# Neighbourhood attention in token tiles of 16 rows x 8 columns in a hybrid encoder block

## The chip, the core and the metric

The kernel runs on one core of a Trainium2 chip. Its engines are TensorE (PE in the profile, its weight loads PEld), VectorE (DVE), ScalarE (ACT), GpSimd (POOL) and SyncE (SP), which here only issues transfers. The metric is the time of one execution on the device in microseconds (us), the median of several runs.

## The reference

One layer of an encoder is applied to two groups of tokens with shared weights: a prompt of 1024 tokens (a grid of 16 rows x 64 columns) and a sample of 256 tokens (4 rows x 64 columns), 1024 features each. What matters here:

```python
kh = min(NA_KH, rows)                     # 8 of the 16 rows; all 4 of the sample
row_start = jnp.clip(r - kh // 2, 0, rows - kh)
key_rows = row_start[:, None] + jnp.arange(kh)[None, :]
col_start = jnp.clip(c - NA_KW // 2, 0, GRID_W - NA_KW)      # 16 of the 64 columns
in_win = (c[None, :] >= col_start[:, None]) & (c[None, :] < col_start[:, None] + NA_KW)
s = jnp.einsum('rqhd,rikhd->hrqik', qg, kg).astype(jnp.float32) * scale + bias
s = jnp.where(mask, s, -jnp.inf)
```

So a token attends to 8 rows x 16 columns around it, in 8 heads of 64, with a learned bias by relative row and column. The second half of the features goes through differential attention (4 heads, every token sees every token of its group, with a T5 bucketed bias by the distance of the token numbers). Both halves are normalised per head, concatenated and multiplied by `w_out`; then follow a mixture of 16 experts, each of which takes the tokens with the best router values (128 of the prompt, 32 of the sample), and a last norm.

## The kernel before

The work is written by hand as one program per engine with semaphores between them; the order on each engine is the order of the code. Tokens are handled in tiles of 128: tiles 0 to 7 are the prompt, 8 and 9 the sample. In the kernel before, a prompt tile is two grid rows of 64 columns, so tile t is tokens 128t to 128t + 127.

Stages: (1) x tiles are loaded, normalised (VectorE), turned (TensorE transposes) and the values of the neighbourhood heads are projected; (2) neighbourhood attention, steps s = 0 to 39, step s = job s // 10 (two heads), tile s % 10; (3) the values of the differential heads are projected; (4) differential attention, steps 40 to 79; (5) `w_out`, the second norm and the router, tile by tile; (6) choice of tokens for each expert; (7) the 16 experts, from about 865 us to the end.

A step s of stage 2 on TensorE is: `scores(s)` (three matmuls for each head, queries and keys split into a high and a low part; L709), `values(s - 2)` (L747), half of a projection part of the next job (`project_part`, L644 to L646), the transposes of the exponentials of step s - 1 (`turn_exps`, L639), the other half of the projection part, and one transpose of an output (`out_turn`). VectorE adds the bias and takes the maximum (`na_bias`, `bias_max`, L1525), ScalarE takes the exponential (L1173), copies the transposes out (L1184), and rounds a finished projection part (`proj_round`, L1152), which VectorE then splits (`proj_lows`, L1507). The parts share one PSUM bank, so the next part's first matmul waits for that split. Parts of 512 columns end at tiles 1, 3, 6 and 8, parts of 256 at tiles 4 and 9.

The window of a tile is in `na_window`: 512 keys for tiles 0, 1, 6 and 7, 576 for tiles 2 to 5 (nine grid rows), 256 for the sample. The bias of two heads stands in a table TE (128 partitions x 2 heads x 16 rows x 64 columns), read with an offset by the tile; a second form TI serves the tiles with 576 keys. A table is loaded by SyncE in four transfers from the DRAM tensor `bias_rows` (`na_table`, L537), and GpSimd adds the column mask and makes TI (`bias_tables`, L1970 to L1980). The T5 bias is one row of 2047 values for each head; GpSimd writes it to DRAM 128 times, each shifted by one (`t5_shifted`, L2024), and SyncE loads one table of 128 x 1920 for each head (`df_table`, L540).

SyncE's queue is one list: weights of a projection (`unit`, tile `w_st`, one buffer, L503; each waits until the one before it is split) and the tables, in the order of the code. In stage 5 SyncE loads for each tile the x rows (L577) and the mixed rows (L580), and GpSimd stores the residual and the normalised rows (L2088, L2090). In stage 6 TensorE counts the places of the chosen tokens with bf16 matmuls (`count`, L897).

## Time and profile before

| | us |
|---|---|
| median of three runs | 2776.01 (2773.64 to 2778.3) |
| the profiled execution | 2778.91 |
| its span | 2777.2 |

| engine | busy us | share | instructions |
|---|---|---|---|
| TensorE, matmuls | 2681.3 | 97% | 22988 |
| TensorE, weight loads | 2524.0 | 91% | 22988 |
| VectorE | 1979.2 | 71% | 2352 |
| ScalarE | 1716.1 | 62% | 2562 |
| GpSimd | 1110.5 | 40% | 745 |

Busy times of engines overlap, so they don't add up to the span. A matmul's duration in the trace reaches over the start of the next one, since matmuls are pipelined; what one costs is read from start to start. The experts take about 1912 us of the span, the neighbourhood attention (stage 2) 237 us.

### The profile page before, as it was taken

Reading aid. Unit: us, or ns where it says so; the run is one execution under the profiler, and the core shown is the slowest. Engines: PE = TensorE matmul, PEld = TensorE weight load, DVE = VectorE, ACT = ScalarE, POOL = GpSimd, SP = SyncE. Lnnn points to the kernel's source line nnn. Section 1 sums busy time; section 2 is a strip of 40 time slices with the busy share of each in tenths; the row PEclk is TensorE's granted clock in tenths of the full one; section 3 lists DMA queues with packets and bytes.
Section 4 is the critical chain, followed back from the end, with each engine's and each line's share of the span. In section 5 each row is a group of like instructions: output and inputs, shape, how many; then the busy total and the mean of one; then the engine's idle time right before and its main releaser. Section 6 shows DMA issues by size and latency. Waiting matters only on the chain. (4 is left out here: it accounts for less than half of the span.)

```text
span 2777.2 us, 54444 instructions
## 1 busy us (share of the span) xinstructions
PE 2681.3 (97%) x22988; PEld 2524.0 (91%) x22988; DVE 1979.2 (71%) x2352; ACT 1716.1 (62%) x2562; POOL 1110.5 (40%) x745
## 2 busy tenths in 40 slices
PE   7999999998986999999999999999999999999997
PEld 7887898877876999999999999999999999999997
DVE  5233326666367878878788787888878788787877
ACT  3366615555114676767667676676767767676675
POOL 2132220124112443636446273552635436263455
PEclk9999999999997999999999999999999999999999
DMA  7231110113364888889887898879889888898987
GB/s 188 54 101 40 48 55 30 40 56 102 127 239 143 316 289 316 285 318 315 290 325 265 318 316 308 317 267 342 285 310 323 287 307 286 318 316 305 320 284 290
DMA packets 357643, 655.40 MB, mean 236 GB/s; under 512 B 25751, under 2 KB 85015, under 8 KB 356887
## 3 DMA queue, kind: packets, MB, share of 16 engines
q1 hardware_dynamic: 341291, 606.41, 61.4%
q0 software_dynamic: 16112, 45.53, 6.1%
q8 instruction: 183, 3.00, 0.4%
q14 instruction: 57, 0.47, 0.0%
HBM read 616.48 MB, written 39.62 MB: 236 GB/s over the span
## 5 line engine op out<-in xcount | busy, mean ns | idle before, releaser
L1798 DVE TENSOR_TENSOR wl<-stg,wh 128x2048 bf16<-128x2048 f32 (+1 forms) x544 | 1244.3, 2292 | 270.4 <-ACT wh L1312 265.7
L1312 ACT ACTIVATE wh<-stg 128x2048 fp32r<-128x2048 f32 (+1 forms) x544 | 1010.9, 1861 | 204.4 <-PE S L958 77.9
L2160 POOL TENSOR_TENSOR hx<-hh,hx 128x320 fp32r<-128x320 f32 x176 | 385.1, 2188 | 811.7 <-ACT hx L1365 811.5
L955 PE MATMUL S<-X,wh 128*128 128x320 f32 x3760 | 593.1, 313 | 1.3 <-DVE X L1807 1.3
L955 PEld LDWEIGHTS S<-X,wh 128*128 128x128 f32 x3760 | 557.5, 189 | 3.9 <-issue 2.1
L1001 PE MATMUL S<-hx,wh 128*128 128x320 f32 x1892 | 312.4, 313 | 5.3 <-DVE yTs L1846 5.2
L955 PE MATMUL OG<-X,wh 128*128 128x320 f32 x1872 | 298.5, 312 | 0.7 <-DVE gg L1828 0.7
L958 PE MATMUL S<-Xb,wl 128*128 128x160 bf16 x3760 | 290.1, 233 | 0.0
L1001 PEld LDWEIGHTS S<-hx,wh 128*128 128x128 f32 x1892 | 280.7, 188 | 7.4 <-issue 7.1
L955 PEld LDWEIGHTS OG<-X,wh 128*128 128x128 f32 x1872 | 277.2, 188 | 2.1 <-issue 1.9
L958 PEld LDWEIGHTS S<-Xb,wl 128*128 128x128 bf16 x3760 | 258.9, 98 | 12.0
L2162 POOL CAST hb<-hx 128x320 bf16<-128x320 f32 x176 | 206.1, 1171 | 0.0
L1365 ACT ACTIVATE hx<-hh 128x320 fp32r<-128x320 f32 x176 | 83.1, 472 | 176.3 <-DVE hh L1835 176.3
L1999 POOL TENSOR_TENSOR ca<-lsum,half 128x20 f32<-128x20 f32 (+3 forms) x10 | 24.2, 2420 | 395.1 <-ACT o_all L1205 242.5
L1001 PE MATMUL OG<-hx,wh 128*128 128x320 f32 x924 | 158.0, 313 | 1.9 <-DVE yTs L1846 1.9
L958 PE MATMUL S<-hb,wl 128*128 128x160 bf16 x1892 | 158.8, 233 | 0.0
L1173 ACT ACTIVATE E<-E,nmax 128x1024 f32<-128x1024 f32 (+1 forms) x80 | 81.8, 1023 | 109.9 <-DVE nmax L1525 109.9
L644 PE MATMUL OG<-hT_h,wkq 128*128 128x512 f32 (+1 forms) x384 | 149.2, 388 | 0.1
L958 PE MATMUL OG<-Xb,wl 128*128 128x160 bf16 x1872 | 149.2, 233 | 0.0
L1001 PEld LDWEIGHTS OG<-hx,wh 128*128 128x128 f32 x924 | 138.7, 188 | 2.5 <-issue 2.5
L958 PEld LDWEIGHTS S<-hb,wl 128*128 128x128 bf16 x1892 | 132.1, 98 | 8.1
L646 PE MATMUL OG<-hT_h,wkq 128*128 128x512 f32 (+1 forms) x384 | 136.8, 356 | 0.0
(287 smaller groups left out, 4277.5 us busy)
## 6 DMA issues: line engine op xcount, KB each, us to landing
stg<-in_w_gate_dram SPq DMA_DIRECT2D x80, 2048.0 KB, 8.7
stg<-in_w_up_dram SPq DMA_DIRECT2D x80, 2048.0 KB, 9.5
stg<-in_w_down_dram SPq DMA_DIRECT2D x64, 2048.0 KB, 12.0
stg<-in_w_down_dram SPq DMA_DIRECT2D x32, 1536.0 KB, 11.4
stg<-in_w_gate_dram SPq DMA_DIRECT2D x16, 1024.0 KB, 5.2
stg<-in_w_up_dram SPq DMA_DIRECT2D x16, 1024.0 KB, 5.2
w_st<-in_w_in_dram SPq DMA_DIRECT2D x20, 512.0 KB, 3.7
yt<-mixed SPq DMA_DIRECT2D x10, 512.0 KB, 4.5
```

Of the source, the lines that this page charges most:

```text
L644: pe.matmul(out, lhs_h, rhs_h, start=first, stop=False)
L646: return pe.matmul(out, lhs_l, rhs_h, start=False, stop=last)
L955: pe.matmul(out, w, x, start=first, stop=False, skip_group_check=True)
L958: return pe.matmul(out[:, 0:CT], w, x, start=False, stop=last, skip_group_check=True)
L1001: mm = pe.matmul(down_bank(e, d), whk[:, f, c * P:(c + 1) * P], hx[:, f0 + f, :], start=(f0 + f == 0), stop=(last and f0 + f == FT - 1), s ...
L1173: act.activation(e, e, ACT.Exp, scale=-1.0, bias=nmax[:, col:col + 1], accum_out=lsum[:, j % 2, t, hf:hf + 1]).then_inc(exp_done, 1)
L1312: act.activation(piece_conv(wh, g), piece_stage(g), ACT.Copy).then_inc(rounded, 1)
L1365: act.activation(hx[:, j - 1:j + 1, 0:CT], hh[:, :, :], ACT.Copy).then_inc(hidden_hi, 1)
L1798: dve.tensor_tensor(piece_conv(wl, g), piece_stage(g), piece_conv(wh, g).bitcast(F32), ALU.subtract).then_inc(split, 1)
L1999: own(pool.tensor_tensor(a, ls, minus_one, ALU.pow))
L2160: pool.tensor_tensor(hx[:, f, CT:2 * CT], hh[:, :, :], hx[:, f, 0:CT].bitcast(F32), ALU.subtract).then_inc(hidden_ready, 1)
L2162: pool.tensor_copy(hb[:, f, :], hx[:, f, 0:CT].bitcast(F32)).then_inc(hidden_b, 1)
```

## The change

Prompt tiles are cut another way: tile t is the 16 rows of the grid by the 8 columns 8t to 8t + 7, so partition 8r + c holds row r, column 8t + c. The 16 columns that a token attends to lie in its own tile and the two beside it, so a window is 384 keys for tiles 1 to 6 and 256 for tiles 0 and 7. The sample keeps its tiles. All layouts of prompt tokens follow: x rows are loaded and the residual and normalised rows are stored by these tiles (`octet`, `octet_of`), the two DRAM tensors stay in the token order.

- Bias of the neighbourhood heads: `na_table` now loads, for each head, two pieces TS for the sample (64 x 6 x 64) and 16 pieces TR, one for each query row (8 partitions x 8 x 24), 36 transfers a table. GpSimd masks TS and makes from TR five blocks TB (left, own, right tile, with and without a column mask for the outer ones).
- Bias of T5: GpSimd reads the T5 rows back as 32 partitions of 2040, puts them into the new order with 15 copies of 32 x 248 (`t5_w`) and stores them in 8 transfers (`t5_octets`). `df_table` loads 16 pieces for each head, one for each grid row. The shifted table stays for the sample alone, much smaller (`df_sample_table`). VectorE's first bias waits for the 8 stores too, since `t5_w` lies under its output.
- VectorE makes one more mask (`window_mask`): five small operations more in the load stage.
- Mixed rows: `mixed_rows(t)` issues the mixed rows as soon as their buffer is free, and the x rows behind them, each with a semaphore of its own; before, x rows stood ahead and both waited for `x2_ready`.
- Choice of tokens: the counting on TensorE uses two more matrices (`row_le`, `row_lt`) so that equal router values go in token order; 32 count matmuls instead of 18. `list_constants` on GpSimd makes them, and the token numbers of the new tiles.
- Weights of the projection (5, 0) are now loaded before the wait for the values of stage 3.

Cut to its core, the diff is:

```diff
 def na_window(t):
     if t >= TPR:
-        return TPR, NSA, 7 - 2 * (t - TPR), False
-    if t < 2:
-        return 0, 512, 7 - 2 * t, False
-    if t < 6:
-        return t - 2, 576, 3, True
-    return 4, 512, 3 - 2 * (t - 6), False
+        return TPR, NSA
+    first, last = max(t - 1, 0), min(t + 1, TPR - 1)
+    return first, (last - first + 1) * P
...
             def na_table(j):
                 for hh_ in range(2):
+                    q = (2 * j + hh_) * NDR
                     for up in range(2):
-                        q = (2 * j + hh_) * NDR
-                        src = G_d[:, q:q + NDR, GW - 1:2 * GW - 1]
-                        sp.dma_start(TE[j % 2][GW * up:GW * up + GW, hh_, up:up + NDR, :], src).then_inc(te_in[j % 2], 16)
+                        sp.dma_start(TS[j % 2][GW * up:GW * up + GW, hh_, :, :],
+                                     G_d[:, q + 5 - up:q + 11 - up, GW - 1:2 * GW - 1]).then_inc(te_in[j % 2], 16)
+                    for r in range(GR):
+                        r0 = row_start(r)
+                        d0 = q + r0 - r + NA_KH - 1
+                        sp.dma_start(TR[j % 2][OC * r:OC * r + OC, hh_, r0:r0 + NA_KH, :],
+                                     G_d[0:OC, d0:d0 + NA_KH, GW - 1 - OC:GW - 1 + 2 * OC]).then_inc(te_in[j % 2], 16)
             def df_table(h):
-                sp.dma_start(BT[h % 2][:, :], Fs_d[h, :, P - 1:P - 1 + 1920]).then_inc(bt_in[h % 2], 16)
+                for r in range(GR):
+                    sp.dma_start(BT[h % 2][OC * r:OC * r + OC, :].rearrange("c (g q) -> c g q", q=P),
+                                 W_d[h, :, :, GR - 1 - r:2 * GR - 1 - r, :].rearrange("c g r k -> c g (r k)")
+                                 ).then_inc(bt_in[h % 2], 16)
...
             def mixed_rows(t):
+                if t < 2:
+                    x_again(t)
                 if t >= 2:
                     sp.wait_ge(turned, wo_fill["y", t - 2] + 2)
-                    sp.wait_ge(x2_ready, t - 1)
-                sp.dma_start(xt[:, t % 2, :], x_rows(t)).then_inc(y_in[t % 2], 16)
                 if t % 4 == 0:
                     sp.wait_ge(y_rest_stored[t // 4], 16)
                 sp.dma_start(yt[t % 2][:, :], y_d[t * P:(t + 1) * P, :]).then_inc(y_in[t % 2], 16)
+                if t >= 2:
+                    x_again(t)
...
             def window_mask():
                 dve.wait_ge(const_ready, 1)
+                dve.wait_ge(ident_ready, 1)
+                own(dve.tensor_tensor_reduce(msk_j[:, :], identf[:, :], msk_c[:, :], 1.0, 0.0, ALU.mult, ALU.add,
+                                             col_of[:, :]))
+                own.wait()
+                own(dve.tensor_tensor(from_col[:, :], msk_c[:, 0:OC], col_of[:, :].to_broadcast([P, OC]), ALU.is_ge))
+                own.wait()
+                dve.tensor_scalar(mask_lr[:, 0, :], from_col[:, :], -MASKED, MASKED, ALU.mult, ALU.add)
+                dve.tensor_scalar(mask_lr[:, 1, :], from_col[:, :], MASKED, 0.0, ALU.mult, ALU.add)
...
+            for g in range(2 * TPR - 1):
+                own(pool.tensor_copy(t5_w[:, g, :, :], t5_x[:, OC * g:OC * g + (2 * GR - 1) * GW].rearrange(
+                    "q (r w) -> q r w", w=GW)[:, :, 0:OC]))
+            own.wait()
+            for c in range(OC):
+                pool.dma_start(W_d[:, c].rearrange("h g r k -> h (g r k)"),
+                               t5_w[OC - 1 - c:DF_H * OC:OC].rearrange("q g r k -> q (g r k)")).then_inc(W_out, 16)
...
+            for t in range(TPR):
+                if t + 1 < TPR:
+                    n = TPR - t - 1
+                    count(ranks[:, 0, t + 1:TPR, :], one, chosen[:, 0, t, :].unsqueeze(1).to_broadcast([P, n, NE]))
+                    count(ranks[:, 1, t + 1:TPR, :], row_le, chosen[:, 1, t, :].unsqueeze(1).to_broadcast([P, n, NE]))
+                if t:
+                    count(ranks[:, 1, 0:t, :], row_lt, chosen[:, 1, t, :].unsqueeze(1).to_broadcast([P, t, NE]))
+                count(ranks[:, 1, 0:TPR, :], one, chosen[:, 0, t, :].unsqueeze(1).to_broadcast([P, TPR, NE]))
```

How this moves instructions, at three places. First TensorE in stage 2, from the end of one step to the values of the next, in job 0. S is the score bank, OG holds outputs and projections, PT the transposes, En the exponentials, PTs their copies. Before (a step with 576 keys):

```order
L639 MATMUL PT<-identf,En 128x128
L639 MATMUL PT<-identf,En 64x128
L639 MATMUL PT<-identf,oTs 128x128
L709 MATMUL S<-K_h,Qh 128x288 x2
L709 MATMUL S<-K_l,Qh 128x288 x2
L709 MATMUL S<-K_h,Ql 128x288 x2
L709 MATMUL S<-K_h,Qh 128x288 x2
L709 MATMUL S<-K_l,Qh 128x288 x2
L709 MATMUL S<-K_h,Ql 128x288 x2
L747 MATMUL OG<-PTs,V 64x128 x10
```

and now (384 keys):

```order
L689 MATMUL PT<-identf,En 128x128 x6
L694 MATMUL OG<-hT_h,wkq 128x512
L695 MATMUL OG<-hT_l,wkq 128x512
L696 MATMUL OG<-hT_h,wkq 128x512
L694 MATMUL OG<-hT_h,wkq 128x512
L695 MATMUL OG<-hT_l,wkq 128x512
L696 MATMUL OG<-hT_h,wkq 128x512
L689 MATMUL PT<-identf,oTs 128x128
L759 MATMUL S<-K_h,Qh 128x384 x2
L759 MATMUL S<-K_l,Qh 128x384 x2
L759 MATMUL S<-K_h,Ql 128x384 x2
L795 MATMUL OG<-PTs,V 64x128 x6
```

The scores are one group of three pairs, the third group of transposes behind the second half of the projection is gone, and six value matmuls stand for ten.

Second SyncE's queue around the first tables, where `w_st` is the buffer of projection weights. Before:

```order
L503 DMA w_st<-in_w_in_dram 128x8x128 [waits w_split] x2
L537 DMA TE_71<-bias_rows 64x15x64 [waits te_clear,G_out]
L537 DMA TE_71<-bias_rows 64x15x64 x3
L537 DMA TE_72<-bias_rows 64x15x64 x4
L503 DMA w_st<-in_w_in_dram 128x8x128 [waits w_split] x3
```

and now:

```order
L529 DMA w_st<-in_w_in_dram 128x8x128 [waits w_split] x2
L562 DMA TS_73<-bias_rows 64x6x64 [waits te_clear,G_out]
L562 DMA TS_73<-bias_rows 64x6x64
L567 DMA TR_75<-bias_rows 8x8x24 x16
L562 DMA TS_73<-bias_rows 64x6x64 x2
L567 DMA TR_75<-bias_rows 8x8x24 x16
L562 DMA TS_74<-bias_rows 64x6x64 x2
L567 DMA TR_76<-bias_rows 8x8x24 x16
L562 DMA TS_74<-bias_rows 64x6x64 x2
L567 DMA TR_76<-bias_rows 8x8x24 x16
L529 DMA w_st<-in_w_in_dram 128x8x128 [waits w_split] x3
```

Between the same two weight loads stand 72 transfers instead of 8.

Third GpSimd between the store of the T5 rows (`t_rows`) and the first table. Before:

```order
L1956 DMA t_rows<-t_p 4x2048 [waits t5_ready]
L1959 MEMSET TE_71 128x2048 [waits va_split,const_dma]
L1960 MEMSET TE_72 128x2048
L1961 TENSOR_SCALAR slw<-slw 128x128
L1970 TENSOR_TENSOR TE_71<-TE_71,mask 128x2048 [waits pool_own,mask_ready,te_in0]
```

and now:

```order
L2028 DMA t_rows<-t_p 4x2048 [waits t5_ready]
L2031 MEMSET TR_75 128x768 [waits va_split,const_dma]
L2032 MEMSET TR_76 128x768
L2033 TENSOR_SCALAR slw<-slw 128x128
L2042 DMA t_x<-t_rows 32x1x2040 [waits pool_own,squared,F_out,turned]
L2046 COPY t_w<-t_x 32x248 [waits shifts_in]
L2046 COPY t_w<-t_x 32x248 x14
L2050 DMA t_octets<-t_w 4x3720 [waits pool_own]
L2050 DMA t_octets<-t_w 4x3720 x7
L2060 TENSOR_TENSOR TS_73<-TS_73,mask 128x768 [waits te_in0,mask_ready]
```

The read, the 15 copies and the 8 stores stand ahead of the first table's mask.

## Rows read from the trace of the kernel before

**Rows 1.** Stretch: length; busy PE, PEld, DVE, ACT, POOL; clock; DMA share; GB/s.

```profile
112.90:350.30 237.40, 236.32 (x1903) 189.42 (x1902) 74.59 (x203) 153.12 (x520) 58.06 (x42) 1.00 0.21 57
830.00:865.00 35.00, 6.82 (x47) 5.40 (x48) 24.21 (x77) 8.71 (x12) 8.64 (x12) 0.50 0.06 19
```

**Rows 2.** Timeline of TensorE, 131 to 137 us: 576 keys (start, duration, engine, line).

```profile
131.12 1.03 PE L639 MATMUL PT<-identf,En 128*128 128x128 f32 x8
131.91 0.47 PE L644 MATMUL OG<-hT_h,wkq 128*128 128x512 f32 x1
...
133.37 0.38 PE L639 MATMUL PT<-identf,En 128*128 128x128 f32 x2
133.59 0.27 PE L639 MATMUL PT<-identf,oTs 128*128 128x128 f32 x1
133.79 0.40 PE L709 MATMUL S<-K_h,Qh 64*128 64x288 f32 x2
...
134.78 1.46 PE L747 MATMUL OG<-PTs,V 128*64 128x128 f32 x20
136.17 0.38 PE L644 MATMUL OG<-hT_h,wkq 128*128 128x256 f32 x1
```

**Rows 3.** Timeline of TensorE, 224 to 232 us: 256 and 512 keys.

```profile
224.46 0.39 PE L709 MATMUL S<-K_h,Qh 64*128 64x256 f32 x2
...
225.01 1.09 PE L747 MATMUL OG<-PTs,V 128*64 128x128 f32 x16
226.04 0.39 PE L644 MATMUL OG<-hT_h,wkq 128*128 128x256 f32 x1
...
227.57 0.60 PE L639 MATMUL PT<-identf,En 128*128 128x128 f32 x4
227.92 0.36 PE L644 MATMUL OG<-hT_h,wkq 128*128 128x256 f32 x1
...
229.64 0.50 PE L709 MATMUL S<-K_h,Qh 64*128 64x512 f32 x2
...
230.54 0.66 PE L747 MATMUL OG<-PTs,V 128*64 128x128 f32 x8
231.13 0.50 PE L644 MATMUL OG<-hT_h,wkq 128*128 128x512 f32 x1
```

**Rows 4.** Timeline at 121 us: last projection matmul, the next weights' rounding, the split.

```profile
121.30 0.39 PE L646 MATMUL OG<-hT_h,wkq 128*128 128x512 f32 x1
...
122.22 0.62 ACT L1113 ACTIVATE wkq<-w_st 128x512 fp32r<-128x512 f32 x1
...
122.36 0.69 DVE L1507 SCALAR_TENSOR_TENSOR K_l<-OG,K_h 128x512 fp32r<-128x512 f32 x1 [3.15 <-ACT K_h L1152]
```

**Rows 5.** Timeline of SyncE's queue, and landings: KB each, median us to landing.

```profile
35.19 0.43 SPq L526 DMA_DIRECT2D lam_v<-in_lambda_k_dram  x1
...
78.95 9.13 SPq L537 DMA_DIRECT2D TE<-bias_rows  x8
...
167.25 2.84 SPq L537 DMA_DIRECT2D TE<-bias_rows  x4
...
w_st<-in_w_in_dram SPq DMA_DIRECT2D x20, 512.0 KB, 3.7
```

**Rows 6.** Timeline of GpSimd, 50 to 92 us; in brackets idle time and what ended it.

```profile
55.63 0.63 POOL L1956 DMA_DIRECT2D t_rows<-t_p  x1 [8.01 <-DVE t_p L1402]
...
87.50 4.60 POOL L1970 TENSOR_TENSOR TE<-TE,mask 128x2048 f32<-128x2048 f32 x1 [27.11 <-DMA TE<-bias_rows]
```

**Rows 7.** Timeline of VectorE at 34 us, the end of the mask.

```profile
34.37 0.19 DVE L1458 TENSOR_SCALAR mask<-msk_w 128x64 f32<-128x64 f32 x1
```

**Rows 8.** Timeline of TensorE at 846 us, the counts.

```profile
846.43 1.89 PE L897 MATMUL S<-chosen,one 128*128 128x224 bf16 x18
```

**Rows 9.** Timeline of TensorE, 689 to 706 us, transposes of the mixed rows.

```profile
690.29 1.09 PE L639 MATMUL PT<-identf,yt 128*128 128x128 f32 x8 [0.79 <-DMA yt<-mixed]
...
705.48 0.83 PE L639 MATMUL PT<-identf,yt 128*128 128x128 f32 x5 [0.44 <-DVE h2T L1713]
```

More of the change, by code:

```diff
@@ L273, in build @@
     mask = after("mask", [P, GW], F32)
+    mask_lr = after("mask_lr", [P, 2, OC], F32)
+    col_of = after("col_of", [P, 1], F32)
+    from_col = after("from_col", [P, OC], F32)
     ssx = after("ssx", [P, 2 * TT], F32)
@@ L719, in exp_blocks @@
                 nk = na_window(t)[1]
-                return [En[:, 2 * (s % 2) + hf, b * P:min(nk, (b + 1) * P)] for hf in range(2) for b in range(na_blocks(t))]
+                return [En[:, 2 * (s % 2) + hf, b * P:(b + 1) * P] for hf in range(2) for b in range(nk // P)]
             def turn_exps(s, fills):
@@ L899, in _ @@
             count(S[:, 1, 0:2 * TT * NE], tri, chosen[:, :, :, :].rearrange("p m t e -> p (m t e)"), first=True)
[L900 to L906 removed]
+            for t in range(TPR):
[6 more added lines that the diff above has]
+                count(ranks[:, 1, 0:TPR, :], one, chosen[:, 0, t, :].unsqueeze(1).to_broadcast([P, TPR, NE]))
+            for t in range(TPR, TT):
+                if t + 1 < TT:
+                    count(ranks[:, :, t + 1:TT, :], one,
+                          chosen[:, :, t, :].unsqueeze(2).to_broadcast([P, 2, TT - t - 1, NE]))
+                mm = count(ranks[:, 1, TPR:TT, :], one,
+                           chosen[:, 0, t, :].unsqueeze(1).to_broadcast([P, TT - TPR, NE]), last=t == TT - 1)
             mm.then_inc(pos_ps, 1)
@@ L1530, in na_bias @@
                 j, t = s // TT, s % TT
-                _, nk, row, inner = na_window(t)
+                nk = na_window(t)[1]
                 if t == 0:
@@ L1963, in _ @@
             pool.sem_inc(te_clear, 1)
+            pool.wait_ge(F_out, 16)
+            pool.wait_ge(turned, 2 * TT)
+            pool.wait_ge(squared, TT)
+            stand()
+            n = 2 * NPR - OC
+            pool.dma_start(t5_x[:, 0:n], bass.AP(F_d.tensor, F_d.offset, [[2 * NPR, DF_H], [1, OC], [1, n]])
+                           ).then_inc(shifts_in, 16)
+            pool.wait_ge(shifts_in, 16)
+            for g in range(2 * TPR - 1):
+                own(pool.tensor_copy(t5_w[:, g, :, :], t5_x[:, OC * g:OC * g + (2 * GR - 1) * GW].rearrange(
+                    "q (r w) -> q r w", w=GW)[:, :, 0:OC]))
@@ L1970, in bias_tables @@
-                own(pool.tensor_tensor(te, te, mask[:, :].unsqueeze(1).to_broadcast([P, 32, GW]), ALU.add))
-                own.wait()
-                if j:
-                    pool.wait_ge(scores_read, 2 * ((j - 1) * TT + 6))
-                stand()
-                for h in range(2):
-                    own(pool.tensor_copy(TI[:, h, :], TE[j % 2][:, h, 3:12, :].rearrange("p r c -> p (r c)")))
-                own.wait()
-                stand()
-                own(pool.memset(TI[0:GW, :, 8 * GW:9 * GW], MASKED))
@@ L1980, in bias_tables @@
-                own(pool.memset(TI[GW:P, :, 0:GW], MASKED))
+                stand()
+                te = TS[j % 2][:, :, :, :].rearrange("p h r c -> p (h r) c")
+                tr = TR[j % 2][:, :, :, :].rearrange("p h r u -> p (h r) u")
+                own(pool.tensor_tensor(te, te, mask[:, :].unsqueeze(1).to_broadcast([P, 12, GW]), ALU.add))
+                for b, u, side in ((0, 0, None), (1, 0, 0), (2, 1, None), (3, 2, 1), (4, 2, None)):
+                    out = TB[j % 2][:, b, :, :].rearrange("p h (r c) -> p (h r) c", c=OC)
+                    cols = tr[:, :, OC * u:OC * u + OC]
+                    if side is None:
+                        own(pool.tensor_copy(out, cols))
+                    else:
+                        own(pool.tensor_tensor(out, cols,
+                                               mask_lr[:, side, :].unsqueeze(1).to_broadcast([P, 2 * GR, OC]), ALU.add))
@@ L2044, in list_constants @@
                 own(pool.memset(one[:, :], 1.0))
+                own(pool.memset(row_le[:, :], 1.0))
+                own(pool.memset(row_lt[:, :], 1.0))
                 own(pool.memset(posm[:, :, NE:NE + 2], 0.0))
@@ L2063, in list_constants @@
                 own(pool.memset(NG[:, :, NE:NE + 2, 2:PARTS], 0.0))
+                own.wait()
+                for rows, base in ((row_le, OC), (row_lt, 0)):
+                    own(pool.affine_select(out=rows[:, :], in_=rows[:, :], compare_op=ALU.is_gt, fill=0.0, base=base,
+                                           pattern=[[OC, GR], [0, OC]], channel_multiplier=-1))
                 own.wait()
```

139 lines of the change are left out of this document (87 added, 52 removed).

## The prediction

> **What bounds the kernel now.** I read the busy share by stage first, then the matmul queue instruction by instruction, then the queues beside it. The stage of the neighbourhood attention runs from 112.9 to 350.3 us, and TensorE is busy for 236.32 of its 237.40 us at the full granted clock, with VectorE at 74.59, ScalarE at 153.12 and GpSimd at 58.06 [rows 1]. The stage lasts as long as the list of matmuls on TensorE. It holds 40 steps (four jobs of two heads, ten token tiles each). A step is scores, values of the step before last, half a projection part, transposes of the previous step's exponentials, the other half, one transpose of an output. The prices are the distances from one start to the next [rows 2, 3]:
> - Scores: 0.99 us for a window of 576 keys, 0.90 for 512, 0.55 for 256.
> - Values: 1.39 us for five key blocks, 1.03 for four, 0.59 for two.
> - Transposes: 0.79 us for eight blocks, 0.22 more for a third group of two, 0.35 for four.
> - A turned output: 0.20 us.
>
> **The sum on TensorE.** Before, a job has four tiles of 512 keys, four of 576 and two (the sample) of 256. Scores cost 4 x 0.90 + 4 x 0.99 + 2 x 0.55 = 8.66, values 4 x 1.03 + 4 x 1.39 + 2 x 0.59 = 10.86, transposes 4 x 0.79 + 4 x 1.01 + 2 x 0.35 = 7.90: 27.4 us. After, six tiles have 384 keys (three blocks) and four have 256. No row shows 384 keys. I take it halfway between the rows at two and four blocks, since it is as far from either: scores 0.73 (bounds 0.55 and 0.90), values 0.81 (0.59 and 1.03), transposes of six blocks 0.57 (0.35 and 0.79). That makes 6 x 2.11 + 4 x 1.49 = 18.6 us. The difference is 8.8 us a job, **35.2 us** in four. If three blocks cost what two do, the gain is 50; if they cost what four do, it is 20; the block count is even between them, so I keep 2 us on either side. VectorE and ScalarE lose work too (384 columns for 512 and 576), which is worth nothing, as neither is waited for.
>
> **The projection chain becomes the next limit.** A projection part can start when ScalarE has rounded the last one and VectorE has split it. From the last matmul's start at 121.30 that takes until 122.36 + 0.69 = 123.05, which is 1.75 us [rows 4]. What covers it is 0.23 (that matmul) + 0.20 + the scores + the values. Before, by the same prices, it is at least 2.0 after a part of 512 columns (0.43 + 0.55 + 1.03 at tile 9). After, the cover is 0.43 + 0.73 + 0.59 = 1.75 at tile 2, 0.43 + 0.55 + 0.81 = 1.79 at tile 7 and 0.43 + 0.55 + 0.59 = 1.57 at tile 9. With 0.1 for the semaphore that leaves waits of 0.1, 0.05 and 0.25, about 0.4 a job, **+1.6 us** (bounds 0, and 8 if ScalarE is late by the 0.5 us that a further copy puts ahead of the rounding).
>
> **GpSimd's T5 work** (a read back, 15 copies of 32x248, 8 stores) stands ahead of the first table. The T5 rows are stored at 55.6 and GpSimd is then idle until the first table's mask at 87.50 [rows 6]. That mask moves 2048 columns in 4.60 us, so a copy of 248 columns takes at most 0.6, 15 take 9, and 8 stores at the 0.63 of the row take 5. From about 72 us, when the stores ahead of it in that queue are done, plus some 3 us for the read, it ends before 90, and step 0 asks for it at 113. I cost it at nothing; the cover is 20 us wide. A table itself gets cheaper: 768 columns and five of 256 instead of 2048 and more.
>
> **SyncE's queue is the risk.** A bias table was 4 transfers and becomes 36, and the first two tables stand ahead of the weight load w_st that ScalarE rounds in step 1. Let p be the time of one issue. The first table is issued by 79.0 + 36p, lands some 3 us later and takes GpSimd 4 us: ready at 86 + 36p, asked for at 113.6, so p may be 0.76. The weights land at 79.0 + 72p + 3.7 [rows 5] and were rounded at 122.22 [rows 4], after the change at about 121.8, so p may be 0.54. A small transfer (lambda's rows) stands at 0.43, and the old table's at 2.84 / 4 = 0.71 with the queue quiet, at 9.13 / 8 = 1.14 when it was fed faster than it drained [rows 5]. The new ones carry 64 or 384 pieces against the 960 of a TE transfer. They are nearest to the small one, so I take p = 0.5 and **0 us**; above 0.54 each 0.1 costs 7.2 us. The later tables have a whole job ahead of them, and the T5 tables (16 transfers each, for one) lie in stretches of 40 us and more; nothing there.
>
> That pieces land slowly is not seen: the four TE transfers of the first table, 960 pieces of 256 bytes each, were issued from 78.95 on and in place for the mask at 87.50 [rows 5, 6], and a new table has 3584 pieces against 3840.
>
> **Small terms.** VectorE makes a column mask in the load stage, five small operations and two waits of its own; such ones, of 0.19 us each by the row and less apart, are the last thing ahead of the next tile's normalisation [rows 7]; with the waits I count 0.7 for the five. TensorE runs without a gap there, so it goes on the path: **+0.7** (bounds 0 and 5 x 0.19 = 1.0). The rank count grows from 18 small matmuls in 1.89 us [rows 8] to 32; 14 more are 1.5 by number, 0.4 by columns: **+1.0**, at 1.2 GHz, since the granted clock is 0.50 there [rows 1]. The mixed rows no longer wait for x2; the one transpose that waited for them, 0.79 us, goes to the 0.44 that the others wait for VectorE [rows 9]: **-0.4**. So that edit is worth next to nothing. The weights that the first differential step rounds come earlier: **-0.3** at most, an estimate. The differential attention, the values of the second half and the experts keep their work, and the new order of tokens changes no size there.
>
> **The sum.** -35.2 + 1.6 + 0.7 + 1.0 - 0.4 - 0.3 = -32.6 us. The profiled execution took 2778.9 us, with a span of 2777.2, so its span becomes 2744.6. The median of the runs is 2776.0, which gives **2743.4 us**.
>
> **Rivals.**
> - *Queue in part.* p is near the 0.71 of TE's transfers: 72 x (0.71 - 0.54) = 12 us of wait at step 1, 2755 us. For it: the source and the shape in runs are those. Against: fewer pieces, 8 partitions each.
> - *Chain.* ScalarE comes to the rounding late at every part's end, 8 us instead of 1.6: 2750 us. Against it: ScalarE has 153 of 237 us of work before and less after.
> - *Slower.* Each issue takes the 1.14 us of the crowded stretch. Step 1 then waits 72 x 0.60 = 43 us for its weights, and the two later tables, 41 us each, cost 7 each against the 34 us that they have (the next weights are rounded some 7.4 steps of 5.1 us later and take 3.7 to land): 57 us, and 2776.0 - 32.6 + 57 = 2800 us. It decides from p = 0.97 on, where the loss passes 32.6. Against it: that row's pace was set by 960 pieces a transfer.
> - *One behind the other.* If a transfer began only when the one before had landed, at the 3.7 us of w_st, step 1 would wait 72 x (3.7 - 0.54) = 228 us and each of the two later tables cost 133 - 34 = 99: some 3170 us. Four TE transfers went out in 2.84 us, less than one such landing [rows 5], so transfers overlap; I leave it 0.01. The Trainium skill (DMA: Bandwidth & Descriptors, "Anatomy of one DMA — SWDGE (gpsimd) path") has a fixed cost of about 2.0 us in each transfer of GpSimd's path; at that pace in SyncE's queue the time would be 2776 - 33 + 105 + 2 x 38 = 2924 us, an estimate. Those rows 5 speak against it as a pace, whatever one transfer takes by itself.
> - *No effect*, that the stage is held by something other than TensorE: 2776. Rows 1 leave 1 us for it.
>
> **Chances.** My forecast 0.68 (2740 to 2747), chain 0.11, queue in part 0.14, slower 0.03, one behind the other 0.01, no effect 0.03. The range of 2739 to 2755 reaches over both middle rivals and the 2 us on the price of three blocks. Faster by over 0.2% (below 2770.5), which is about what a measurement of this kernel can tell from no change: 0.93; within: 0.03; slower: 0.04.
>
> **What would show it.** In the profile after, the stage of neighbourhood attention lasts some 204 us at a granted clock of 1.00; a step with 384 keys shows scores near 0.73, values near 0.81 and transposes near 0.57 us. Step 0's bias on VectorE starts when its scores end (no wait for the table), and ScalarE's rounding in step 1 does not wait for w_st. Projection parts at tiles 2, 7 and 9 wait a little for VectorE. I am wrong if SyncE's issues are over 0.54 us apart, if three blocks cost like four, or if the stages behind the attention grow.

## The result and the profile after

| | before | after |
|---|---|---|
| median us | 2775.63 (2773.64 to 2778.3) | 2744.11 (2743.25 to 2746.34) |
| the profiled execution | 2778.91 | 2746.34 |
| its span | 2777.2 | 2744.3 |

Both kernels ran four times on the same chip. The ratio is 0.9885, with a 95% interval of 0.9872 to 0.9897: the change takes 31.5 us away. The two spans differ by 32.9 us. By stage, each measured on TensorE from the first matmul of one stage to the first of the next (us):

| stage | before | after | difference |
|---|---|---|---|
| load, to the first scores | 112.90 | 114.31 | +1.41 |
| neighbourhood attention | 238.07 | 205.42 | -32.65 |
| values of the differential heads | 59.32 | 59.32 | 0 |
| differential attention, three jobs | 201.69 | 201.66 | 0 |
| its last job, and up to the first mixed row | 56.24 | 56.26 | 0 |
| `w_out`, norm, router | 176.86 | 176.56 | -0.30 |
| choice of tokens, to the gathers | 5.93 | 6.35 | +0.42 |
| gathers, and the 16 experts to the end | 1926.16 | 1924.40 | -1.76 |

The whole gain lies in the stage of neighbourhood attention. Its row of the windows, in the columns of [rows 1], answers the first of them:

```profile
114.31:319.73 205.42, 202.05 (x1473) 158.76 (x1472) 62.25 (x203) 129.81 (x499) 54.40 (x45) 1.00 0.21 45
```

TensorE is still what the stage waits for, but it is idle for 3.4 us of it now, where it was for 1.4 of the 238.07 (1.1 up to 350.3, where the row of [rows 1] ends). The timeline of TensorE from 130 to 135 us shows a step with 384 keys and answers [rows 2, 3] (start, duration; the price is the distance to the start of the next group):

```profile
130.74 0.82 PE L689 MATMUL PT<-identf,En 128*128 128x128 f32 x6
131.32 0.47 PE L694 MATMUL OG<-hT_h,wkq 128*128 128x512 f32 x1
...
132.98 0.44 PE L759 MATMUL S<-K_h,Qh 64*128 64x384 f32 x2
...
133.71 0.88 PE L795 MATMUL OG<-PTs,V 128*64 128x128 f32 x12
134.51 0.38 PE L694 MATMUL OG<-hT_h,wkq 128*128 128x256 f32 x1
```

Transposes of six blocks are 0.57 us apart from what follows, scores 0.72, values 0.81; these are the medians of the 24 steps with 384 keys, and the single distances above lie within 0.01 of them. SyncE's queue and GpSimd's work ahead of the first table (timelines, answering [rows 5, 6]):

```profile
80.63 1.30 SPq L562 DMA_DIRECT2D TS<-bias_rows  x2
81.97 6.66 SPq L567 DMA_DIRECT2D TR<-bias_rows  x16
...
104.96 5.75 SPq L567 DMA_DIRECT2D TR<-bias_rows  x16
110.75 0.40 SPq L529 DMA_DIRECT2D w_st<-in_w_in_dram  x1
```

```profile
77.03 6.01 POOL L2046 COPY t_w<-t_x 32x248 f32<-32x248 f32 x15 [4.16 <-DMA t_x<-t_rows]
...
97.57 1.85 POOL L2060 TENSOR_TENSOR TS<-TS,mask 128x768 f32<-128x768 f32 x1 [10.06 <-DMA TR<-bias_rows]
```

and the two places that ask for what they bring, VectorE's first bias and ScalarE's rounding in step 1:

```profile
115.17 0.41 DVE L1586 CUSTOM_DVE_ANT_1 En<-S,TB 128x256 f32<-128x256 f32 x1
```

```profile
123.06 0.62 ACT L1166 ACTIVATE wkq<-w_st 128x512 fp32r<-128x512 f32 x1
```

The 72 transfers go out in 110.75 - 80.63 = 30.1 us, 0.418 us each. GpSimd has finished with the T5 rows 10 us before the first table is in place, and the table is ready at 102, 13 us before VectorE asks for it. Neither of the two places waits: no idle time stands in brackets behind them.

### The profile page after: what moved, and what is told of

Same layout as the page of the kernel before. It is cut to its first block and busy times, and to the rows that moved or that the text cites. A ratio compares the mean times of both kernels' runs of the same rounds, so it can differ in the third digit from the quotient of the medians.

```text
span 2744.3 us, 53807 instructions
## 1 busy us (share of the span) xinstructions
PE 2645.4 (96%) x22570; PEld 2492.4 (91%) x22570; DVE 1967.1 (72%) x2357; ACT 1692.1 (62%) x2538; POOL 1110.0 (40%) x781
```

## Experiments

Each kernel is the changed one with the edit shown, if nothing else is said. A ratio is to runs of the kernel before on the same chip; the changed kernel's own is 0.9885. The medians of before were 2776.8 us beside the first four, 2776.55 beside the next four, 2774.58 beside the ninth to eleventh and 2776.95 beside the last. Where nothing was edited, the neighbourhood stage repeats to 0.1 us from profile to profile, the stages next to it to 0.2, and whole executions don't: the first tile's projection, the last job of the differential attention and the experts take some us more or less from one to the next. So the verdicts rest on lengths of stages, each read from one profile of the kernel, and the medians stand beside them. "The last job" is measured from its first scores to the scores of its last step, nine steps on.

**1. A fourth key block.**

```diff
-    first, last = max(t - 1, 0), min(t + 1, TPR - 1)
-    return first, (last - first + 1) * P
+    if t in (0, TPR - 1):
+        return max(t - 1, 0), 2 * P
+    return min(t - 1, TPR - 4), 4 * P
```

> The changed kernel with four key blocks instead of three in prompt tiles 1 to 6 (the bias of the fourth is of another block, so the output is not the reference's). TensorE theory: the price goes with the number of blocks, between the 0.72/0.81/0.57 us of three and the 0.90/1.03/0.79 of four: 24 x 0.62 = +14.9 us, less about 1 us of waits that the longer cover takes away, so about 2758 us against the 2744.1 of the changed kernel. Rival (the stage is held by something that does not count blocks, a table or a queue): within 2 us of 2744.

2759.84 us (ratio 0.9941, 0.9925 to 0.9958). The stage lasted 219.76 us, 14.3 more than 205.42. TensorE's timeline of this kernel:

```profile
141.40 0.50 PE L760 MATMUL S<-K_h,Qh 64*128 64x512 f32 x2
...
142.29 1.09 PE L796 MATMUL OG<-PTs,V 128*64 128x128 f32 x16
...
144.83 1.04 PE L690 MATMUL PT<-identf,En 128*128 128x128 f32 x8
```

Scores cost 0.89 us, values 1.02, transposes 0.79: 0.60 more a tile, 3.6 in a job of six such tiles. The stage is paid by the key block, as the sum had it (14.9 less about 1 were expected).

**2. Transposes twice.** Every transpose of exponentials in the neighbourhood attention is made twice into the same place.

```diff
-                        turn(F_TURN[s] + n, blocks[4 * n:4 * n + 4])
+                        turn(F_TURN[s] + n, blocks[4 * n:4 * n + 4], 2 if s < NAS else 1)
...
-                for m, src in enumerate(blocks):
+                for m, src in [x for x in enumerate(blocks) for _ in range(times)]:
```

> The changed kernel with each transpose of the exponentials in the neighbourhood stage issued twice; nothing is added on any other engine. TensorE theory: 24 x 0.57 + 16 x 0.35 = +19.3 us, about 2763. Rival (ScalarE or VectorE set the step): +0 to 3 us.

2765.96 us (0.9962, 0.9948 to 0.9976). The stage lasted 227.58 us, 22.2 longer, which is the 208 added transposes at 0.107. That is more than the 19.3 expected: twelve transposes in a row are 1.23 us from what follows, so the six added cost 0.66 and not the 0.57 of a group by itself. Work of TensorE goes onto the path in full.

**3. A dose for ScalarE.** Four copies of 128x128 without use stand behind each output copy.

```diff
                 act.activation(o_all[j % 2][:, t, :], PT[:, f % 2, 0:P], ACT.Copy).then_inc(turned_copied, 1)
+                for n in range(4 if s < NAS - 2 else 0):
+                    act.activation(dose[:, n, :], identf[:, :], ACT.Copy)
```

> The changed kernel with four more copies of 128x128 on ScalarE behind the output copies of 38 of the 40 steps, some 1.0 us of its time each. TensorE theory: ScalarE has room, 0 to +2 us. Rival (ScalarE is the next limit): up to +38 us, 2782.

2751.86 us (0.9909, 0.9892 to 0.9925), 7.7 more, where 0 to 2 were expected; the stage lasted 212.40 us, 7.0 longer, and the values behind it 1.5. So ScalarE had less to spare than I thought. The waits are not those of the projection chain, which kept their lengths (0.91 at tiles 7 and 9), but stand ahead of the output's transpose (TensorE's timeline of this kernel, idle time in brackets):

```profile
180.89 0.30 PE L690 MATMUL PT<-identf,oTs 128*128 128x128 f32 x1 [0.71 <-ACT PTs L1238]
...
186.56 0.30 PE L690 MATMUL PT<-identf,oTs 128*128 128x128 f32 x1 [0.22 <-ACT PTs L1238]
```

With 0.91 us of copies in a step, ScalarE copies the transposes out too late at tiles 2 (but for job 0), 3 and 7. At the other tiles the dose costs nothing, except for 0.8 us at the last step of the stage. The forecast "VectorE and ScalarE are not waited for" holds for the change as it is, with a margin below 0.9 us in such steps.

**4. SyncE's queue doubled.** Each TR transfer is cut into two.

```diff
-                        sp.dma_start(TR[j % 2][OC * r:OC * r + OC, hh_, r0:r0 + NA_KH, :],
-                                     G_d[0:OC, d0:d0 + NA_KH, GW - 1 - OC:GW - 1 + 2 * OC]).then_inc(te_in[j % 2], 16)
+                        for g in range(0, NA_KH, 4):
+                            sp.dma_start(TR[j % 2][OC * r:OC * r + OC, hh_, r0 + g:r0 + g + 4, :],
+                                         G_d[0:OC, d0 + g:d0 + g + 4, GW - 1 - OC:GW - 1 + 2 * OC]
+                                         ).then_inc(te_in[j % 2], 16)
```

> The changed kernel with each of the 32 TR transfers of a table cut into two halves, 68 transfers a table instead of 36. Queue theory: at the measured 0.38 us a TR and 0.63 a TS issue, two tables take 53.7 us from 80.6 on, the weights for step 1 are issued at 134.3 instead of 110.8 and land at 138, asked for at about 123: +15 us, 2759. The later tables (26.8 us each against 34) cost nothing. Rival (the queue is never waited for): 0.

2759.52 us (0.9939, 0.9922 to 0.9955), 15.4 more. The stage lasted 222.47 us, 17.0 longer, all of it in job 0 (66.7 us for 49.6). SyncE's queue and ScalarE's timeline of this kernel:

```profile
134.74 11.07 SPq L529 DMA_DIRECT2D w_st<-in_w_in_dram  x2
```

```profile
138.77 0.63 ACT L1168 ACTIVATE wkq<-w_st 128x512 fp32r<-128x512 f32 x1 [14.81 <-DMA w_st<-in_w_in_dram]
```

The 136 transfers took 53.1 us, 0.391 each, and the weights were rounded 14.8 us late. So the queue was the real risk of this change, with the mechanism and the place of the forecast: 64 transfers more are 17 us. What the change itself has left is a margin of 8.5 us: the weights issued at 110.75 are in place 3.8 us later, at 114.56, and ScalarE rounds them at 123.06.

**5. Transposes ahead of the waiting projection part**, at tiles 2, 7 and 9.

```diff
+                early = s >= 2 and s % TT in (2, 7, 9)
+                if early:
+                    turn_exps(s - 1, (0, 1))
                 project_part(s, 0)
-                if s >= 1:
+                if s >= 1 and not early:
                     turn_exps(s - 1, (0, 1))
```

> The changed kernel with the transposes of the exponentials ahead of the first half of the projection part in tiles 2, 7 and 9 of each job. Chain theory: TensorE then does them while it would wait for VectorE's split (0.15, 0.10 and 0.33 us a job beyond the bare price in the changed kernel's trace), so -2.3 us, 2741.8, and the values of those steps no longer show the wait. Rival (the wait only moves to the copies of those transposes): 0.

2743.47 us (0.9874, 0.9858 to 0.9891), no difference that the median shows, but the stage lasted 203.32 us instead of 205.42. First the changed kernel at tile 9, then this one:

```profile
158.90 0.60 ACT L1205 ACTIVATE Qh<-OG 128x512 fp32r<-128x512 f32 x1 [0.72 <-PE OG L696]
...
159.45 0.66 PE L795 MATMUL OG<-PTs,V 128*64 128x128 f32 x8
...
159.53 0.69 DVE L1568 SCALAR_TENSOR_TENSOR Ql<-OG,Qh 128x512 fp32r<-128x512 f32 x1 [2.77 <-ACT Qh L1205]
...
160.36 0.35 PE L694 MATMUL OG<-hT_h,wkq 128*128 128x256 f32 x1 [0.26 <-DVE Ql L1568]
```

```profile
160.18 0.66 PE L795 MATMUL OG<-PTs,V 128*64 128x128 f32 x8
...
160.77 0.66 PE L689 MATMUL PT<-identf,En 128*128 128x128 f32 x4
...
161.18 0.36 PE L694 MATMUL OG<-hT_h,wkq 128*128 128x256 f32 x1
```

In the first, the values are followed after 0.91 us, of which 0.33 is the wait for the split. In the second the transposes stand in that place and nothing waits. Step by step, 0.33 is gone at tile 9 and 0.12 at tile 7 of each job, but at tile 2 only job 0 is shorter (0.30); in the later jobs that step is as long as before.

**6. The column mask later.** VectorE makes it behind the fourth tile's normalisation.

```diff
+                if t == 3:
+                    column_mask()
```

> The changed kernel with the new column mask on VectorE moved from the load stage to the values of the second half of the heads, where VectorE waits 2.46 us a tile. Mask theory: the gap of 0.63 us of TensorE at 37.9 us goes and all behind it starts 0.7 us earlier. Rival (the gap comes from a late x tile): it stays.

One run, 2742.53 us. The gap of 0.63 us at the sixth tile is TensorE's wait in this line of the changed kernel:

```profile
37.91 1.17 PE L689 MATMUL PT<-identf,xin 128*128 128x128 f32 x8 [0.63 <-DVE hT_l L1494]
```

It is gone here: from the transposes of one tile to the next TensorE takes 3.86 us there, as before, against 4.53 or 4.54 in all nine profiles that have the new mask in the load stage. In this and the two later kernels with the same edit, it is 3.85 or 3.86.

**7. x rows in the order of the tokens.** The x rows of a prompt tile are 128 rows in a row, for the attention and for the residual alike.

```diff
-            return prompt.rearrange("(r g c) d -> g r c d", r=GR, c=OC)[t]
+            return prompt[t * P:(t + 1) * P, :]
```

> The changed kernel with x loads and stores of the prompt by 128 consecutive tokens as before (bias and windows stay those of the new tiles, so the output is not the reference's). Row theory: 4 KB pieces take their 159 ns at the median again instead of 246 to 285, the first x tile lands near 4.5 us instead of 6.1, the stages behind start 0.7 us earlier, in all -0.7 to -1.5 us. Rival (chance of that one execution): the pieces take as long as in the changed kernel's trace.

2741.92 us (0.9878, 0.9861 to 0.9894). The issues of the changed kernel, then of this one (KB each, median us to landing), and TensorE's first instruction and first projection of values in each:

```profile
xt<-in_x_prompt_dram SPq DMA_DIRECT2D x8, 512.0 KB, 5.0
...
E<-in_x_prompt_dram SPq DMA_DIRECT2D x4, 512.0 KB, 6.6
```

```profile
9.75 1.94 PE L689 MATMUL PT<-identf,E 128*128 128x128 f32 x8 [9.75 <-DVE E L1529]
...
18.54 0.58 PE L694 MATMUL S<-va_h,hT_h 128*128 128x256 f32 x1 [0.23 <-DVE va_l L1466]
```

```profile
xt<-in_x_prompt_dram SPq DMA_DIRECT2D x8, 512.0 KB, 3.8
...
E<-in_x_prompt_dram SPq DMA_DIRECT2D x4, 512.0 KB, 4.1
```

```profile
8.25 1.94 PE L689 MATMUL PT<-identf,E 128*128 128x128 f32 x8 [8.25 <-DVE E L1529]
...
16.38 0.58 PE L694 MATMUL S<-va_h,hT_h 128*128 128x256 f32 x1 [0.23 <-DVE va_l L1466]
```

A tile of 16 pieces of 32 KB lands later than one piece of 512 KB. In the first 40 us a packet of 4 KB took 159 ns at the median here, as before the change, and 268 in the changed kernel, so the expectation holds and its rival (chance of one execution) doesn't. TensorE's first projection of values starts at 16.4 to 16.7 us in the three profiles with rows in order (before, this one, the eleventh) and at 18.1 to 18.7 in the eleven others: the change pays 1.9 us for it, and I had not priced it at all. In the stage of `w_out`, where the x and mixed rows land later too, it costs nothing (176.55 and 176.56).

**8. The T5 copies eight times.**

```diff
-            for g in range(2 * TPR - 1):
+            for g in 8 * list(range(2 * TPR - 1)):
+                if g == 0:
+                    own.wait()
```

> The changed kernel with the 15 T5 copies on GpSimd made eight times: 48 us instead of 6. Cover theory: 10 us of idle time of GpSimd and some 12 us from the first table to its first use hide the first 22 us, so of the 42 added about 19 to 20 show: the first bias starts at about 134 instead of 115, the time is about 2763. Rival (the table is used later than I think or the order on GpSimd doesn't matter): 0.

One run, 2756.24 us, where 2763 was expected. The stage lasted 219.54 us, 14.1 longer, all in job 0. GpSimd's and VectorE's timelines:

```profile
79.77 43.07 POOL L2048 COPY t_w<-t_x 32x248 f32<-32x248 f32 x120 [4.45 <-DMA t_x<-t_rows]
```

```profile
131.38 0.42 DVE L1586 CUSTOM_DVE_ANT_1 En<-S,TB 128x256 f32<-128x256 f32 x1 [14.93 <-POOLq L2072]
```

VectorE's first bias starts when the table is there, at 131.4 and not at the expected 134. The added copies cost 43.07 - 6.01 = 37.1 us of GpSimd's time instead of the 42 I took, and some 23 of them were covered: 10 us by the wait for TR, the rest by the time until VectorE asks. The total rose by 12.1 only: the last job of the differential attention was 41.37 us here and 44.21 in the changed kernel, 2.8 shorter. That was the next question.

**9. Both small repairs together** (5 and 6).

> Both small repairs together: the transposes stand ahead of the projection part at tiles 2, 7 and 9, and the column mask is made behind the fourth tile's normalisation. Alone the first made the stage of neighbourhood attention 203.32 instead of 205.42 us (-2.1) and the second took a gap of 0.63 us out of the load stage. If they add up: 2744.1 - 2.7 = 2741.4 us. What can blur it is the last job of the differential attention, which lasted 41.4 to 45.2 us in the profiles so far, with the same instructions, by how often the granted clock dropped in it; the rival is that the sum is lost in that.

2740.07 us (0.9874, 0.9857 to 0.9890). The stage lasted 203.28 us, the gap is gone, and the last job took 41.41. The two gains add up to 2.8 us in the trace. The median is 4.0 below the changed kernel's, but the kernel before ran 1.0 faster beside it too; by the ratios it is 3, and their intervals overlap. So what is shown are the 2.8 us in the trace.

**10. The last job filled.** To the kernel of run 9, eight matmuls without use in each step of that job but the first.

```diff
+            def filler(n):
+                pe.wait_ge(fill_split, CHUNKS * JOBS8)
+                for _ in range(n):
+                    pe.transpose(G[:, 0:P], identf[:, :], identf[:, :])
...
             for s in range(LAST, STEPS):
+                if s > LAST:
+                    filler(4)
                 scores(s)
+                if s > LAST:
+                    filler(4)
```

> The kernel of the run before, and in the last job of the differential attention four matmuls of 128 columns without use ahead of each step's scores and four behind them, where TensorE waits for VectorE (36.5 of 44.2 us busy in the changed kernel). Theory: the granted clock drops there because TensorE stands idle between the pieces, so it stays at 1.00, and the job takes 41.4 us, as in the profiles without a drop, plus what of the 9 x 8 x 0.11 = 8 us stands where TensorE isn't idle: between 2738.6 and, if half of it does, 2742.6; I take 2739.5. Rival: the drops don't come from idleness; the job then takes 44 us and more, 2741.4 to 2749.

2739.68 us (0.9872, 0.9855 to 0.9888), the same as run 9. The windows of the last job, in the columns of [rows 1], of the changed kernel, of run 9 and of this one:

```profile
580.71:624.92 44.21, 36.24 (x266) 29.54 (x265) 38.81 (x62) 32.94 (x71) 18.47 (x17) 0.92 0.35 123
```

```profile
578.80:620.20 41.40, 33.45 (x265) 27.08 (x264) 36.35 (x62) 32.62 (x71) 19.34 (x17) 1.00 0.38 131
```

```profile
578.14:621.60 43.46, 40.30 (x333) 34.09 (x332) 36.86 (x61) 32.33 (x70) 20.28 (x17) 1.00 0.36 125
```

Filled, the clock stayed at 1.00 up to the first mixed row. But the filling cost 2.1 us in the job and gave back 2.2 behind it (9.85 us to the first mixed row instead of 12.09). Most of the 2.2 is the clock: in the kernels without filling that stretch took 12.0 to 12.1 us at a granted clock of 0.86, in nine profiles, and 10.4 at 1.00, in four. It decides little on the cause, since run 9, not filled, had 1.00 in the job as well, and so had runs 1, 4 and 8. The first row shows something else: VectorE is busy for 2.5 us more in the long job, with the same instructions.

**11. Mixed rows alone.** The kernel before with that edit.

```diff
                 if t >= 2:
                     sp.wait_ge(turned, wo_fill["y", t - 2] + 2)
-                    sp.wait_ge(x2_ready, t - 1)
-                sp.dma_start(xt[:, t % 2, :], x_rows(t)).then_inc(y_in[t % 2], 16)
                 if t % 4 == 0:
                     sp.wait_ge(y_rest_stored[t // 4], 16)
                 sp.dma_start(yt[t % 2][:, :], y_d[t * P:(t + 1) * P, :]).then_inc(y_in[t % 2], 16)
+                if t >= 2:
+                    x_again(t)
```

> The kernel before with one edit of the change alone: mixed rows ahead of the x rows, each with a semaphore of its own. The prediction has 0.4 us for it, at the one transpose that waited for the mixed rows. Stage 5 was 176.97 us before (first transpose of mixed rows to the threshold of the choice) and 176.6 to 176.7 in every kernel with the change. Expected: 176.6 here too, 0.3 less in all, 2775.8 us, which is no difference that can be timed. Rival: the x rows, now later, hold up the residual sum, and the stage is longer than 177.

2773.48 us, ratio 0.9992 (0.9983 to 1.0002): no difference. The stage took 176.61 us instead of 176.86. So -0.3 us is the whole worth of the edit. (The expectation's 176.97 and 176.6 to 176.7 start one matmul, 0.11 us, ahead of the first mixed row.)

**12. GpSimd's products in pieces.** The trace shows one thing that lengthens the last job. The changed kernel, VectorE and GpSimd from 598 us on, and TensorE behind them:

```profile
598.48 2.91 POOL L2102 TENSOR_TENSOR o_all<-o_all,slw 128x1280 f32<-128x1280 f32 x1
598.64 3.84 DVE L1651 SCALAR_TENSOR_TENSOR A<-E,cf 128x1024 f32<-128x1024 f32 x1
```

```profile
602.54 1.10 PE L689 MATMUL PT<-identf,A 128*128 128x128 f32 x8 [2.31 <-DVE A L1651]
```

and the same place in run 9:

```profile
596.16 1.43 DVE L1661 SCALAR_TENSOR_TENSOR A<-E,cf 128x1024 f32<-128x1024 f32 x1
...
596.59 3.79 POOL L2112 TENSOR_TENSOR o_all<-o_all,slw 128x1280 f32<-128x1280 f32 x1
```

VectorE's product takes 1.28 us elsewhere. Here it takes 3.84, and its end, 602.48, is 1.1 us behind the end of GpSimd's (601.39): it stood still until GpSimd was done. Where VectorE began first, GpSimd's product took 3.79 instead of 2.91. The Trainium skill (SBUF — State Buffer, "SBUF: two separate sides") states the rule: VectorE and GpSimd share one pair of ports, and of a VectorE instruction with two inputs in SBUF and a GpSimd instruction, whichever starts first holds it to its end. The trace agrees for these wide products, with these durations. It doesn't for GpSimd's narrow power of 128x20: VectorE's product of the weights, with two inputs in SBUF, ran inside it at its usual 0.69 us (changed kernel).

```profile
174.78 3.58 POOL L2087 TENSOR_TENSOR ca<-lsum,half 128x20 f32<-128x20 f32 x1 [56.96 <-ACT o_all L1251]
...
175.15 0.69 DVE L1480 TENSOR_TENSOR wkq<-w_st,wkq 128x512 fp32r<-128x512 f32 x1 [0.40 <-ACT wkq L1166]
```

Nor was VectorE's bias held up, which reads the scores from PSUM: 1.22 us beside a product of GpSimd (596.99 us in the changed kernel) as elsewhere. GpSimd's product begins 17.8 us after the job in both; VectorE's at 17.4 us in the one and 17.9 in the other. The same meeting stands in the two jobs before, in each of the thirteen profiles so far, that of the kernel before too (changed kernel):

```profile
531.88 1.37 DVE L1651 SCALAR_TENSOR_TENSOR E<-E,cf 128x1024 f32<-128x1024 f32 x1
...
532.25 3.79 POOL L2102 TENSOR_TENSOR o_all<-o_all,slw 128x1280 f32<-128x1280 f32 x1
...
533.17 3.42 DVE L1480 TENSOR_TENSOR wkq<-w_st,wkq 128x512 fp32r<-128x512 f32 x1
```

```profile
538.93 0.51 PE L759 MATMUL S<-K_h,Qh 64*128 64x512 f32 x2 [0.65 <-DVE nmax L1586]
...
541.58 2.05 PE L801 MATMUL OG<-V,PTs 128*128 128x128 f32 x16 [1.00 <-ACT PTs L1237]
```

GpSimd's product waits for VectorE's first one, and then VectorE's product of the weights, which takes 0.69 us at other places, waits for GpSimd's. TensorE loses 0.65 and 1.00 us to it. The edit:

```diff
-                own(pool.tensor_tensor(y, y, w[:, :].unsqueeze(1).to_broadcast([P, n, wide]), ALU.mult))
+                for m in range(0, n, step):
+                    own(pool.tensor_tensor(y[:, m:m + step], y[:, m:m + step],
+                                           w[:, :].unsqueeze(1).to_broadcast([P, step, wide]), ALU.mult))
```

and the product ahead of it in the same way, with a fifth of the tokens as the step.

> The changed kernel, with GpSimd's two products over o_all (128x1280, 2.33 and 2.91 us) each cut into five of 256 columns. In the last job of the differential attention the third product of VectorE over A lasted 3.84 to 4.00 us instead of 1.28 in the profiles of before, of the changed kernel and of the one with the transposes ahead, and in each of them it had begun 0.10 to 0.16 us after GpSimd's product had; where VectorE began first, it took 1.4 and GpSimd's took 3.8 instead of 2.9. Theory: the two can't run together, and whoever comes second waits to the end of the other's instruction. Then no product over A is longer than 1.28 + 0.6 us, the last job takes at most 42.4 us instead of 44.2, and the time is 2741.8 us instead of 2744.1. If it is only the granted clock of TensorE that makes that job long, the 3.84 us stay, or the job stays near 44, and the time at 2744.

2740.77 us (0.9868, 0.9851 to 0.9884), 3.3 less than the changed kernel; the intervals of the two ratios overlap, so again the trace decides. VectorE in this kernel at the same places:

```profile
532.29 1.10 DVE L1480 TENSOR_TENSOR wkq<-w_st,wkq 128x512 fp32r<-128x512 f32 x1
```

```profile
595.38 1.44 DVE L1651 SCALAR_TENSOR_TENSOR A<-E,cf 128x1024 f32<-128x1024 f32 x1
```

The three jobs of differential attention, in the changed kernel and in this one:

```profile
379.05:580.71 201.66, 198.05 (x1360) 163.23 (x1360) 128.18 (x237) 114.71 (x284) 25.96 (x18) 1.00 0.20 37
```

```profile
379.87:578.05 198.18, 197.84 (x1359) 163.20 (x1359) 123.57 (x237) 114.94 (x284) 29.18 (x34) 1.00 0.19 37
```

The granted clock is 1.00 in both, and the three jobs took 201.66 to 201.84 us in all thirteen profiles without the edit, so 3.5 us are the meeting of the two engines: 1.8 in each of the two jobs that have it, where the expectation had looked at the last job alone. The last job took 41.97 instead of 44.21, and how that splits is not shown. In the four other profiles at a clock of 1.00 and without filling, VectorE's product took 1.4 us and the job 41.4; in the three at 0.96 (runs 2, 6 and 11) the product took 1.4 and the job 42.2 to 42.4; in the four at 0.92 (both kernels, runs 5 and 7) the product took 3.6 to 4.0 and the job 44.2 to 44.3. Run 3 stands by itself (0.85, 2.3 and 45.2). So one drop of the clock goes with some 0.9 us, and a long product with 1.9 more. But in those four a second drop follows right behind the long product: in the changed kernel TensorE is busy for 0.22 us from 600 to 602, and the clock is at 0.50 from 604 to 606. What of the 1.9 us is the wait and what is that drop, no run separates.

## Why the prediction was right, point by point

The forecast was 2743.4 us, in a range of 2739 to 2755, and the median is 2744.11.

- *TensorE's list bounds the stage.* Right: 35.2 us by the prices, and the stage lost 32.65 with the waits. Runs 1 and 2 show it, as added work of TensorE came out in full.
- *Three blocks halfway between two and four.* Taken 0.73, 0.81, 0.57; measured 0.72, 0.81, 0.57. The doubt of 2 us on either side was not needed.
- *The projection chain, +1.6.* Right in mechanism and place (tiles 2, 7 and 9), a little small: 0.15, 0.10 and 0.33 us instead of 0.1, 0.05 and 0.25, about 2.3 in four jobs. Run 5 took 2.1 us out of the stage with an order of instructions alone, though at tile 2 in job 0 only.
- *The queue, p = 0.5 and nothing lost.* The choice of the nearest row was right: p is 0.418, near the 0.43 of the small transfer. The rivals "queue in part" and "slower" needed 0.71 and 0.97, the crowded stretch's 1.14 did not come back with small transfers, and "one behind the other" is out. Run 4 shows that the threshold is real: with 136 transfers the weights come 14.8 us late.
- *GpSimd's T5 work hidden, cover 20 us wide.* It ends at 87.5, before 90 as said, and it is 10 us ahead of TR's landing. Run 8 found the edge: 23 us of added copies were free and 14 were not. My price of a copy, 0.6, was too high: 0.40.
- *Column mask, +0.7.* Measured 0.68, from 3.86 to 4.54 us at the sixth tile.
- *Count, +1.0.* Too large: +0.42 from the threshold to the first gather. Of my two ways to cost it, by number 1.5 and by columns 0.4, the second was right; I took the mean.
- *Mixed rows, -0.4.* Measured -0.3, alone as well (run 11).
- *Weights earlier, -0.3.* Not seen: the differential attention starts as before (59.32 us of values ahead of it in both), and its first job takes 65.5 us in both.
- *What I left out.* The strided x tiles, +1.9 us until the first projection. I wrote that pieces which land slowly are not seen, and looked at the pieces of the bias table alone; the x rows are on the path from 0 us on. This was a missing term. In the two profiles it showed as +0.7, since the first tile's projection takes 3.5 to 4.95 us from run to run (3.61 in the one of after, 4.72 in the one of before). Its groups of three matmuls start 0.64 us apart at first and 0.36 from some point on; 0.64 stands there five times in the profile of before and once in that of after, at a granted clock of 1.00 in both.
- *The experts, -1.7,* are no effect of the change. From their first matmul to the end it took 1908.2 to 1911.3 us in the twelve kernels with the change (1910.85 in the changed kernel itself), 1912.6 in the kernel before, and 1910.8 in run 11, whose code is that of the kernel before there.

So the typical sum is -32.65 + 1.9 + 0.68 + 0.42 - 0.3 = -30.0 us, where the forecast was -32.6 and the medians say -31.5 (-28.6 to -35.5 by the interval of the ratio). That the forecast came within 0.7 us of the median is in part luck: the missing 1.9 and the 0.7 too little for the chain were only in part made up by 0.6 too much for the count, and the rest lies within the spread of whole executions. What stays open is what ends the slow distances in the first tile's projection, and what the fastest combination would give: the edits of runs 9 and 12 took 2.8 and 3.5 us out of stages at different places, and were not run together.

## What to carry to other kernels

Where one engine's list sets a stage, price it block by block from distances between starts, then ask which chain the shorter list uncovers, for that is where the next 2 us stand and where moving one group in front of a wait recovers them. Count the issues in a queue ahead of a transfer that someone needs, take their pace from the row whose transfers are nearest in the number of pieces, and price every transfer whose layout changes, the very first ones above all. When a stage differs between executions of the same code, look for a single instruction that lasts three times its usual time, and for what the other engine held at its start.

## What the hardware showed that I had not expected

- Wide products of VectorE and GpSimd with two operands in SBUF don't overlap: 0.69 us became 3.42 and 1.28 became 2.33 to 4.00 on VectorE, or 2.91 became 3.79 on GpSimd, by which began first. A power of 128x20 on GpSimd (3.58 us) held nothing up. With GpSimd's products cut into pieces of 256 columns, VectorE's took 1.44 for 1.28, 1.10 for 0.69 and 2.81 for 2.28.
- A transfer of 512 KB in 16 runs of 32 KB, 256 KB apart, landed after 5.0 us instead of 3.8 (xt), and after 6.6 instead of 4.1 (E).
- Small transfers went out of SyncE's queue 0.38 us (TR, 64 pieces, 16 in 6.13 us) and 0.63 us (TS, 384 pieces, two in 1.25) apart; the trace has no landings for them.
- The granted clock of TensorE dropped to half for short stretches in the last job of the differential attention, where TensorE is busy for 36 of 44 us, at other places from run to run, and not in the job when it was filled, but not in five of the others either. Whether idle time alone decides that, these runs don't show.
